# A decoder-layer kernel: the next pair's turning put behind the down product, and its copies behind the down product's copy

## The reference

```python
    def expert_block(args):
        xb, gb = args
        h = jax.nn.silu(jnp.einsum('td,edf->tef', xb, w_gate)) * jnp.einsum('td,edf->tef', xb, w_up)
        h = h * gb[..., None].astype(h.dtype)
        return jnp.einsum('tef,efd->td', h, w_down)
```

## Time and profile before

| what | value |
|---|---|
| median of 3 runs (lowest to highest) | 1051.57 us (1051.37 to 1053.03) |
| the profiled execution's own time | 1052.49 us |
| its span, first to last instruction | 1050.6 us |
| TensorE busy | 955.5 us, 91% of the span |
| TensorE weight loads | 566.8 us, 54% |
| VectorE busy | 531.5 us, 51% |
| GpSimd busy | 327.7 us, 31% |
| ScalarE busy | 234.4 us, 22% |
| moved by DMA | 291.98 MB, 278 GB/s over the span |

### The profile page before, as it was taken

How to read it: one execution, slowest core, us unless ns; L and a number is a source line. 1 busy time by engine, 2 the same in 40 slices (tenths; PEclk the granted TensorE clock), 3 DMA queues, 4 the chain that set the end, 5 groups by cost and what they waited for, 6 DMA issues and landing times.

```text
span 1050.6 us, 18183 instructions
## 1 busy us (share of the span) xinstructions
PE 955.5 (91%) x7418; PEld 566.8 (54%) x7418; DVE 531.5 (51%) x1061; ACT 234.4 (22%) x486; POOL 327.7 (31%) x362
## 2 busy tenths in 40 slices
PE   5999999999999997599999888988999999998995
PEld 4878877877787786348534333333333333332331
DVE  2158957875986688767133312121323223346665
ACT  3241134113412611423111111111111111111013
POOL 0049906960993399000111101110100110124210
PEclk9999999999999999799999999998999999999998
DMA  8645244525434347188699999999999999999951
GB/s 232 179 121 192 102 135 141 186 88 148 161 120 125 91 149 293 26 338 363 240 407 419 420 418 419 421 420 415 410 414 419 415 413 416 416 414 415 364 208 43
DMA packets 87359, 291.98 MB, mean 278 GB/s; under 512 B 17085, under 2 KB 48383, under 8 KB 62424
## 3 DMA queue, kind: packets, MB, share of 16 engines
q1 hardware_dynamic: 72647, 254.03, 63.0%
q0 software_dynamic: 14624, 36.74, 9.2%
HBM read 275.48 MB, written 32.63 MB: 293 GB/s over the span
## 4 chain that ended last, share of the span: by engine, by line
PE 66%; DMA 20%; DVE 8%; issue 3%; ACT 2%; SPq 1%; POOL 0%; DVEq 0%; POOLq 0%
PE bank L1359 63%; DMA big<-in_w_up 11%; DMA big<-in_w_down 5%; ACT big L1656 2%; DMA big<-yrows,big 2%; PE bank L596 1%; DVE big L1946 1%; DMA big<-in_w_in 1%; PE bank L627 1%; DVE big L1057 1%; DVE big L1999 1%; DVE big L991 1%; DVE big L2003 0%; ACT L1656 0%; DVE big L1154 0%
## 5 line engine op out<-in xcount | busy, mean ns | idle before, releaser
L1359 PE MATMUL bank<-big 64*64 64x64 f32 (+8 forms) x6930 | 890.4, 355 | 74.1 <-DVE big L991 17.9
L1359 PEld LDWEIGHTS bank<-big 64*64 64x64 f32 (+5 forms) x6930 | 510.6, 147 | 406.2 <-issue 313.1
L1656 ACT ACTIVATE big<-bank 128x512 f32<-128x512 f32 (+7 forms) x286 | 123.4, 453 | 652.7 <-PE bank L1359 389.4
L1160 POOL DMA_INDIRECT big<-xg,big x32 | 32.9, 1028 | 405.2 <-PE bank L596 327.2
L2150 POOL TENSOR_SCALAR big<-big 128x256 f32<-128x256 f32 x120 | 132.1, 1102 | 1.7
L982 DVE TENSOR_TENSOR big<-big,bank 128x256 f32<-128x256 f32 x32 | 13.5, 421 | 184.3 <-ACT big L1656 184.3
L2162 POOL TENSOR_TENSOR big<-big 128x256 f32<-128x256 f32 x120 | 94.3, 785 | 0.3
L1946 DVE SCALAR_TENSOR_TENSOR big<-big 128x256 f32<-128x256 f32 x120 | 80.1, 668 | 4.1
L991 DVE COPY big<-bank 128x512 f32<-128x512 f32 x32 | 22.1, 690 | 93.5 <-PE bank L1359 93.5
L1656 ACT ACTIVATE big<-big 128x272 f32<-128x272 f32 (+9 forms) x108 | 49.8, 505 | 43.7 <-DVE big L1881 11.3
L1656 ACT ACTIVATE big<-bank,big 128x272 f32<-128x272 f32 (+2 forms) x53 | 23.8, 476 | 111.8 <-PE bank L1359 111.8
(11 more groups left out here) (164 smaller groups left out, 443.7 us busy)
## 6 DMA issues: line engine op xcount, KB each, us to landing
big<-in_w_gate SPq DMA_DIRECT2D x64, 1024.0 KB, 16.6
big<-in_w_up SPq DMA_DIRECT2D x64, 1024.0 KB, 24.4
big<-in_w_down SPq DMA_DIRECT2D x64, 1024.0 KB, 28.0
big<-in_w_in SPq DMA_DIRECT2D x29, 1024.0 KB, 5.5
yrows<-big POOLq DMA_DIRECT2D x32, 512.0 KB, 3.5
big<-in_w_out SPq DMA_DIRECT2D x2, 2048.0 KB, 16.1
big<-in_state_wkv SPq DMA_DIRECT2D x32, 64.0 KB, 2.2
out_wkv_s<-big SPq DMA_DIRECT2D x32, 64.0 KB, 3.9
```

Source lines behind the costliest of these rows:

```text
L1160: pool.indirect_dma_start(out=x[0:n, :], out_offset=None, in_=xg, in_offset=bass.IndirectOffsetOnAxis(ap=idxu[0:n, col:col + 1], axis=0), ...
L1359: return nc.tensor.matmul(out_, lhsT=lhsT, rhs=rhs, start=start, stop=stop)
L1656: return nc.scalar.activation(out_, in_, f, **kw)
```

## The change

In iterations 1 to 30, TensorE's `down(q - 1)` is put ahead of `turn(q + 1)`, and ScalarE's `store(q - 1)` ahead of `turned(q + 1)`. No instruction is added or taken away; VectorE's, GpSimd's and SyncE's programs stay as they are. Iterations 0 and 31 stay as they are too.

```diff
@@ -702,10 +702,10 @@
                 if q == NPAIR - 1:
                     down(q - 1)
                 gate_up(q, 4, KT)
+                if 0 < q < NPAIR - 1:
+                    down(q - 1)
                 if q + 1 < NPAIR:
                     turn(q + 1)
-                if 0 < q < NPAIR - 1:
-                    down(q - 1)
             combine(NPAIR - 2)
@@ -822,10 +822,10 @@
                 if q == 4:
                     act.wait_ge(S['cnt_ready'], 1)
                     count = act.value_load(cnti[0:1, 0:1])
+                if 0 < q < NPAIR - 1:
+                    store(q - 1)
                 if q + 1 < NPAIR:
                     turned(q + 1)
-                if 0 < q < NPAIR - 1:
-                    store(q - 1)
             hidden_turned(NPAIR - 1)
```

## The result

The changed kernel takes 1054.41 us in the median of 20 runs (1050.76 to 1058.27), the kernel before 1051.11 in 20 runs (1048.39 to 1053.25). The ratio is **1.0028, 95% interval 1.0019 to 1.0038**: slower by 2.9 us, within the range. The forecast was 4.85 us. A second set of 12 runs beside 33 of the kernel before gave 1054.69 and 1.0028 again (1.0013 to 1.0042).

What follows compares the result with a forecast made beforehand. Weight DMA bounds most of the expert stage; the end hangs on GpSimd's gather and fetch ahead of `combine(27)`. Terms 0 + 0 + 0.8 + 3.65 + 0.4 = 4.85 us on the 1051.57 median gave 1056.4 us, range 1053.0 to 1058.8.

Steps and rivals of the forecast that it cites:

- The copies behind the turning: ScalarE's copies of the turned rows, now behind everything, stay covered: 0, at most 0.2 us in each of about six iterations.
- rival C: Much slower: the copies show in every iteration from 740 us, 3.6 us on top, 1060.0 us in all; chance 0.08.
- The stall ahead of `combine`: TensorE's wait ahead of `combine`, then begun 5.64 us behind `gate_up` instead of 5.78: taken as 0.
- The cover over `w_down`: The turning no longer hides the landing of `w_down` ahead of the down product: one loss of 0.8 us.
- The gather of i = 30: On GpSimd, gather, fetches behind it, `take(27)` and `combine(27)` all move later by the down product, 3.65 us.
- the store behind the gather: On GpSimd, the last store goes out about 0.6 us later, delaying the first five fetches: nothing lost, or up to 0.5.
- The clock: TensorE's longer gap ahead of `combine(27)`, about 7.6 us, slows the products behind it: 0.4 us more.
- Rival A: No measurable change: later fetches find an emptier queue, the third landing by 969.3; 1053.2 us; chance 0.14.
- Rival B: Faster: the stall ahead of `combine` shrinks by 0.9 us, twice from 898 to 931 us; 1049.8 us; chance 0.05.

Runs made afterwards that it cites:

- e1: Kernel before with the new order in iterations 1 to 24 only, the old one from 25 on: 1050.76 us, ratio 1.0000.
- e12: The changed kernel run again, nothing altered, against the kernel before: 1054.69 us, ratio 1.0028.
- e11: The changed kernel with the old order in iterations 25 and 27 alone: 1055.11 us, ratio 1.0033 to the kernel before.
- e4: Kernel before with the new order in iteration 27 alone: 1053.45 us, ratio 1.0019.
- e5: The changed kernel with GpSimd's store of pair i-4 put ahead of the gather of pair i: 1056.93 us, ratio 1.0061 to the kernel before.
- e9: The changed kernel with store of pair i-4 and fetches of i = 30 and 31 ahead of the gathers: 1051.38 us, ratio 1.0011 to the kernel before.
- e10: Kernel before with the new order in iterations 1 to 24 and fetches of i = 30 and 31 ahead of the gathers: 1047.70 us, ratio 0.9966.
- e7: Kernel before with only the fetches of i = 30 and 31 put ahead of the gathers: 1049.05 us, ratio 0.9983.

## Why the prediction was right, and where its sum was not

The sign, the range and the size hold (2.9 us against 4.85). That the size does is in part luck: 4.05 us of the forecast hung on one gap of 7.6 us ahead of `combine(27)`, which didn't come in the changed kernel, and a late store with a clock that fell more often made up for much of it. Term by term:

1. *The copies behind the turning, 0.* Right. Iterations without `combine` didn't grow: from the end of `gate_up(15)` to the next `turn_hidden` it is 8.85 us after (748.56 to 757.41) and 9.03 before (751.82 to 760.85); rival C (the copies, not the clock) is out.
2. *The stall ahead of `combine`, 0.* Right in kind: released by ScalarE, at 5.47 behind the end of `gate_up` against my 5.64 and 5.78 before (766.89 less 761.42, which is 757.84 and the 3.58 that 16 products take). The small rest came from products in one row, 32 in 7.09 where two times 16 take 3.65 each. Two pairs without a wait for weights now take 31.33 us (735.56 to 766.89) instead of 31.83 (738.82 to 770.65 before). That this is what makes up for the lost cover fits the positions of `combine(25)` under e1, but no run takes it alone.
3. *The cover over `w_down`, 0.8.* The waits came in kind: of those forecast near 797, 830 and 862 us, one of 1.06 at 795.57 and one of 0.62 at 859.33, none near 830. (The prediction's 0.9 to 1.0 for the first was already too much by its rows: 797.5 less 796.71 is 0.8.) The price was mis-sized: `combine(25)` is 0.2 us late from T in the changed kernel, 0.4 in e12, 0.5 early in e1, and 0.0 late in the mean of nine profiles. I had taken the landings as fixed and left out what term 2 gives back. It can still be 0.75 us in one run (e11).
4. *The gather of i = 30, 3.65.* The step that failed is the sentence that everything up to `take(27)` moves with it. The gather did go out 3.64 later; but the fetch landed 2.39 later, not 3.65 (967.70, from 952.30 and 15.4, less 501.00, against 967.24 less 502.93), and `combine(26)` was late by itself, so that the fetch was there 0.1 us before it was needed and the gap shrank. Alone (e4) the late gather makes `combine(27)` 2.54 late, where the term has 3.65. The term that took its place is the one I had bounded by 0.5: "nothing lost, or up to 0.5" for the store behind the gather. It moved the first fetches by 1.85 and `combine(26)` by 2.08. I had counted the issue of the store, 0.6 later, which was 0.12 earlier from T, and not that its landing grows from 8.1 to 10.1 us with a gather 1.3 us ahead of it, nor that the fifth fetch had hardly any slack (it had landed 15.8 us behind its issue at 932.54, at 948.34, and its sum began about then). The fit of the Trainium skill's page "DMA: Bandwidth & Descriptors" (anatomy of one DMA on the gpsimd path), 3.2 us for such a fetch, didn't hold in any profile: beside the weights the first eight fetches, all of 128 rows, took 7.5 to 17.9 us over the 14 profiles.
5. *The clock, 0.4.* Wrong in place and size. I forecast one gap of 7.6 us; it came in e4 and e5 (6.83 and 7.18), where the products behind it took 10.11 and 10.02, 0.5 to 0.6 more than before, as priced. In the changed kernel there was none, but three slow stretches, 2.66, 1.51 and 1.50 us against one of 1.51 before: 4.2 more where I had 0.4. The rule of the Trainium skill ("TensorE: Matmul & The Clock Gate", part 1) is that the slow clock is the default and activity lifts it; the trace agrees in kind, as each of the three stretches begins right behind a gap (3.74, 1.79 and 1.79 us).

The distances close: `combine(25)` is 0.21 late from T and `combine(26)` 1.87 more. From there to `combine(27)` the slow clock adds 2.66, the shorter gap gives back 2.17, and products in one row 0.15: 0.34 more. To `combine(28)` both kernels have a slow stretch: 0.01. To `combine(29)` the changed one alone: 1.50. Together 3.93, of which 0.01 is lost again by the last `combine`.

Rival A (the third fetch lands by 969.3) was missed by little: 466.70 from T, which is 969.6 on the axis of the profile before. Of the 1.3 us by which the fetch moved less than its term, 1.0 is a shorter landing (15.4 us instead of 16.4), as A has it, and 0.3 is GpSimd's way from the gather to the third fetch. Rival B's saving ahead of `combine` was 0.3 and not 0.9. The range's upper end, 1058.8, is 0.2 above the 1058.6 that the bounds gave, for no stated reason; the result lies well inside either.

## What to carry to other kernels

When a step is moved, follow each queue that it releases up to the landing of what stands in it, not to its issue: an indirect transfer with another right ahead of it took 2 us more. A late transfer that another late one hides is found only when they are taken one at a time: alone the late store cost 0.75 us and the late gather 3.15, together the gather hardly showed, and taking the store's delay away (e5) brought the gather's out in full. And where the clock may fall, a count over several profiles tells more than one profile does.

## What the runs showed of the hardware that I had not expected

TensorE's clock fell behind gaps of 1.78 to 1.86 us in 11 of 23 cases when transposes came just before, each time at a cost of 1.5 to 1.65 us, and in none of 20 behind gaps of 1.42 to 1.73 us when large products did. The same kernel had three slow stretches from `combine(26)` on in one profile and four in another. That this alone spreads the times isn't shown: the twelve runs of e9 cover 9.4 us and those of e10, whose gaps there all lie behind products, 4.5, but those of e7, whose gaps do too, cover 8.8. And of two indirect transfers issued 1.3 us apart, the second landed 10.0 to 10.2 us behind its issue and the first 7.8 to 8.4, in either order, in eight profiles.
